# One 512-column product per high weight block: both token parts side by side in the up projections of a split-precision FFN

## The chip, the cores and the metric

The kernel runs on one core of one Trainium2 chip. The metric is the device time of one execution in microseconds (us), lower is better. One number is the median of three runs of the kernel before.

## The reference

Two networks of two layers each run one after the other on one sequence of 256 tokens with model width 1024, all in float32. What matters here are the feed-forward parts:

```
def swiglu(x, w_in, w_out):
    gate, up = jnp.split(x @ w_in, 2, axis=-1)
    return (jax.nn.silu(gate) * up) @ w_out
...
for i in range(DEPTH):                      # first network, DEPTH = 2
    h = x + 0.5 * swiglu(rms_norm(x, norm_ffn1[i]), w_ffn1_in[i], w_ffn1_out[i])   # 1024 -> 2 x 2816 -> 1024
    ... attention and convolution mixer ...
    h = h + 0.5 * swiglu(rms_norm(h, norm_ffn2[i]), w_ffn2_in[i], w_ffn2_out[i])
    ... embedding gate ...
...
for layer in range(DEPTH):                  # second network
    ... three mixers ...
    u = rmsnorm(x, ln2_g[layer]) @ w_up[layer]                                     # 1024 -> 4096
    x = x + jnp.square(jax.nn.relu(u)) @ w_down[layer]                             # 4096 -> 1024
```

So there are four gated feed-forward parts (called ffn1 and ffn2 in each of two layers) and two squared-relu ones (up2 and its down projection).

## The kernel before

**Split precision.** Every large product is made from rounded operands (fp32r) in three pieces: a weight block is split into a high part `whi` and a rest `wlo`, an activation into `x_hi` and `x_lo`, and the product is the sum of `wlo*x_hi`, `whi*x_lo` and `whi*x_hi` in PSUM. The fourth piece, `wlo*x_lo`, is left out.

**Pieces of weight.** The weights arrive as a list of pieces in a fixed order (`plan()`, `NUM[piece]`), mostly 1 MB: four 128-row chunks of 512 columns. The SP queue loads piece n into `raw` (4 buffers). ScalarE makes `whi` of it in `high()` (L998) and VectorE makes `wlo` by a subtraction in `low()` (L1510), both into 4 buffers, three pieces ahead of TensorE (`AHEAD = 3`); `high()` of piece n waits until TensorE has used piece n-4. The order of the work on each engine is written out by hand in the same sequence of stages, and semaphores tie the engines together: `s_used` counts pieces that TensorE has used, `s_hi` and `s_lo` the split ones.

**Up projection.** `columns_` (L520 to L522) takes a 128x128 weight block as the stationary operand and 256 columns (all the tokens) of the transposed activation as the moving one. For each of four chunks of a piece and each of four blocks m it issues the three products, each of 256 columns, into half a bank of PSUM. A unit j consists of two pieces (chunks 0 to 3 and 4 to 7) and fills the two banks of one pair: in the gated parts the first bank holds 2x256 columns of the gate, the second the same of the up value. There are 11 units j in each gated part, and 8 units in each of the two up2 stages (two halves `hf` of 4). The pairs `G0` and `G1` take turns; the pair `P2` and the first bank of `SO` serve as scratch for transposes (`spare`), and the second bank of `SO` for attention values and convolution.

**Behind a unit.** In a gated part VectorE multiplies the gate bank with the row scales (L1610, `s_gate`), ScalarE applies Silu (L1064, `s_silu`), VectorE multiplies with the up bank (L1612, `s_up`); later ScalarE writes `hid_hi` (L1069) and VectorE `hid_lo` (L1618). These instructions stand in the queues between the splits of later pieces. In up2 ScalarE takes the relu out of PSUM (L1422), squares it into `hid_hi` (L1430), and VectorE squares it again (L2136) and subtracts (L2138).

**Down projection and all else.** `rows` (L469 to L471) has the activation as the stationary operand and 512 weight columns as the moving one, in three products as well. The down projections and most of the mixers use it.

**The first stage** has one job more: `bias_of_heads`, a generator that both TensorE and VectorE advance by one at each tick, makes a table (product at L579, VectorE L1592) that goes through a scratch tensor in HBM and returns as `bias` in eight transfers (L2288).

Of the kernel before, what the change touches and what calls it, by code (L numbers as in the profile page):

```python
# [23 lines left out]
AHEAD = 3  # L24
# [152 lines left out]

def hv(name, l, g, t):

    n = NORM[name, l]  # L180
    return 4 * (n - 1) + 4 * ((n > 9) + (n > 11)) + 2 * g + t + 1
# [57 lines left out]
def build(nc, x_d, w_d, c_d, c2_d, rb_d, oh_d, msk_d, pt_d, line_d, out_d):  # L239
    with ExitStack() as ctx:  # L240
# [10 lines left out]
        x_hi = sb("x_hi", [128, 8, 256], F32R)  # L251
        x_lo = sb("x_lo", [128, 8, 256], F32R)
# [38 lines left out]
        PS = [ctx.enter_context(nc.psum_tensor(f"ps{i}", [128, 512], F32)) for i in range(8)]  # L291
        BANKS = {"G0": (PS[0], PS[1]), "G1": (PS[2], PS[3]), "P2": (PS[4], PS[5]), "SO": (PS[6], PS[7])}
        TB = (PS[4], PS[5], PS[6])
        O = PS[7]

# [11 lines left out]
        s_gate, s_silu, s_up, s_hhi, s_hlo = (sem(n) for n in ("s_gate", "s_silu", "s_up", "s_hhi", "s_hlo"))  # L307

        s_relu, s_r2, s_uhi, s_ulo = (sem(n) for n in ("s_relu", "s_r2", "s_uhi", "s_ulo"))
# [22 lines left out]
        s_dv = sem("s_dv")  # L332

# [87 lines left out]
        def tensor(e):  # L421
# [108 lines left out]

            X = (x_hi, x_lo)
# [41 lines left out]
            def bias_of_heads():  # L573

                for _ in range(8):
                    yield
# [5 lines left out]
            def ffn1(l, f, nxt):  # L582
# [11 lines left out]
                for j in range(11):  # L594
                    if j > 1:
                        columns_(u[j][0], bank(f, l, j), f, l)
                    columns_(u[j][1], bank(f, l, j), f, l, mid=(lambda: spread(f, l)) if j == 0 else None)
                    gate_frees(j)
# [320 lines left out]
            def ffn2(l, nxt):  # L919
                H = (F2["hid_hi"], F2["hid_lo"])  # L920
                for hf in range(2):
# [4 lines left out]
                    def relu_frees(j):  # L926
                        free[bks[j]] = [[(s_relu, 2 * (Q + j) + i + 1)] for i in range(2)]

                    columns_(u[0][0], bks[0], "up2", l)
                    if hf == 0:  # L930
                        x_of_h("up2", l, 1)
                    columns_(u[1][0], bks[1], "up2", l)
                    for j in range(4):
                        if j > 1:
                            columns_(u[j][0], bks[j], "up2", l)
                        columns_(u[j][1], bks[j], "up2", l)
                        relu_frees(j)
                    for g in range(2):
                        bk = bks[4 + g]
# [30 lines left out]
        def scalar(e):  # L970
# [84 lines left out]
            def ffn1(l, f, nxt):  # L1055
# [9 lines left out]

                def hid(j):
# [14 lines left out]
                for j in range(11):  # L1081
                    if j > 1:
                        high(NUM[u[j][0]] + AHEAD)
                        hid(j - 1)
                        high(NUM[u[j][1]] + AHEAD)
                    else:
# [92 lines left out]
            def mixer1(l, nxt):  # L1179
# [52 lines left out]
                def sum_turns(g):  # L1232
                    for i in range(2):
# [3 lines left out]
                        e.activation(flat(x_hi[:, c:c + 2, :]), TB[b][:, :], ACT.Copy, scale=0.5).then_inc(s_xhi, 1)  # L1237
# [76 lines left out]
            def x_of_mix(l, c, m):  # L1314
# [3 lines left out]
                e.activation(flat(op[0][:, i:i + m, :]), TB[b][:, 0:256 * m], ACT.Copy,  # L1318
# [92 lines left out]
            def ffn2(l, nxt):  # L1411
                for hf in range(2):
# [3 lines left out]
                    def relu(j):  # L1416
                        for i in range(2):
                            sq = tmp[:, (j % 2) * 1024 + i * 512:(j % 2) * 1024 + i * 512 + 512]
# [3 lines left out]
                            e.activation(sq, BANKS[bank("up2", l, 6 * hf + j)][i][:, :], ACT.Relu).then_inc(s_relu, 1)  # L1422

                    def hid(j):
                        for i in range(2):
# [4 lines left out]
                            e.activation(flat(F2["hid_hi"][:, 4 * j + 2 * i:4 * j + 2 * i + 2, :]), sq, ACT.Square).then_inc(s_uhi, 1)  # L1430
# [4 lines left out]
                    high(NUM[u[1][0]] + AHEAD)  # L1435
                    high(NUM[u[0][1]] + AHEAD)
                    relu(0)
                    high(NUM[u[1][1]] + AHEAD)
                    hid(0)
                    relu(1)  # L1440
                    for j in (2, 3):
                        high(NUM[u[j][0]] + AHEAD)
                        hid(j - 1)
                        high(NUM[u[j][1]] + AHEAD)
                        relu(j)
# [35 lines left out]
        def vector(e):  # L1481
# [52 lines left out]
            def x_low(name, l, lo, hi, T, g, upto):  # L1534

                lo, hi = flat(lo), f32(flat(hi))
# [49 lines left out]
            def bias_of_heads():  # L1586
                for _ in range(8):
# [4 lines left out]
                e.tensor_tensor(T1["line"][:, :], TB[b][0:8, :], T1["msk"][:, :], ALU.add).then_inc(s_lw, 1)  # L1592

            def ffn1(l, f, nxt):
# [6 lines left out]
                def gated(j):  # L1601
                    buf = (j % 2) * 1024
                    gt, pr = tmp[:, buf:buf + 512], tmp[:, buf + 512:buf + 1024]
                    ps = BANKS[bank(f, l, j)]
                    e.wait_ge(s_used, NUM[u[j][1]] + 1)
# [4 lines left out]
                    e.tensor_tensor(two(gt), two(ps[0][:, :]), rsb2, ALU.mult).then_inc(s_gate, 1)  # L1610
                    e.wait_ge(s_silu, 11 * F + j + 1)
                    e.tensor_tensor(pr, ps[1][:, :], gt, ALU.mult).then_inc(s_up, 1)  # L1612
# [508 lines left out]
            def ffn2(l, nxt):  # L2121
# [4 lines left out]
                for hf in range(2):  # L2126
                    Q = 8 * l + 4 * hf
                    u = [halves("w_up_2", l, cols(4 * hf + j)) for j in range(4)]

                    def hid(j):  # L2130
                        for i in range(2):
# [4 lines left out]
                            v = step(e.tensor_tensor(sq, sq, sq, ALU.mult))  # L2136
                            e.wait_ge(s_dv, v)
# [5 lines left out]
                    low(NUM[u[1][0]] + AHEAD)  # L2143
                    low(NUM[u[0][1]] + AHEAD)
                    low(NUM[u[1][1]] + AHEAD)
                    hid(0)
                    for j in (2, 3):
                        low(NUM[u[j][0]] + AHEAD)
                        hid(j - 1)
                        low(NUM[u[j][1]] + AHEAD)  # L2150
                    for g in range(2):
# [8 lines left out]
                        for t in range(2):  # L2160
                            residual(spec, bank("up2", l, 6 * hf + 4 + g), lambda t: rsq(n, t), *nxt, g, back=4 * (hf == 0), ts=(t,))
# [229 lines left out]
```

## Time and profile before

| what | value |
|---|---|
| median of three runs | 1805.46 us (1803.58, 1805.46, 1805.49) |
| profiled execution | 1803.1 us, its span 1801.3 us |
| granted TensorE clock over the span | 0.998 |
| TensorE products (PE) busy | 1780.1 us, 99% |
| TensorE weight loads (PEld) busy | 1617.7 us, 90% |
| VectorE (DVE) busy | 1106.3 us, 61% |
| ScalarE (ACT) busy | 891.7 us, 50% |
| HBM read | 300.02 MB |

The span goes from the first to the last instruction of the profiled execution; 1.8 us of its time lie outside. PE is TensorE's product instructions, PEld its weight loads, which overlap the products. The end of a product in the trace is modelled and products overlap each other in it, so the distance from one start to the next tells what a product costs, and the duration of one row doesn't. A group row gives instructions xcount, busy us, mean ns of one, and the idle time of the engine just before them with what ended it.

### The profile page before, as it was taken

The numbers are of one execution on the slowest core, as the hardware profiler recorded it, in microseconds if no ns is written. First come the engines' busy times: TensorE is split into PE (matmuls) and PEld (weight loads), VectorE is DVE, ScalarE is ACT, GpSimd is POOL, SyncE is SP. The second block draws the span as 40 slices with busy tenths as digits, with TensorE's granted clock in tenths as the row PEclk, the third lists the DMA queues.
The fourth block names the chain that finished last, engine by engine and source line by source line (L and its number), as shares of the span: only waits on it lengthen the run. The fifth ranks groups of instructions, "written<-read, shape, count | busy, mean of one in ns | idle before, by whom it ended". The sixth has DMA issues, their size and how long they took to land.

```text
span 1801.3 us, 28974 instructions
## 1 busy us (share of the span) xinstructions
PE 1780.1 (99%) x11422; PEld 1617.7 (90%) x11422; DVE 1106.3 (61%) x1604; ACT 891.7 (50%) x1304; POOL 26.5 (1%) x32
## 2 busy tenths in 40 slices
PE   9999999999999999999999999999999999999998
PEld 9998898899988999888889998888898988889896
DVE  6555588765555655468775554667565656756554
ACT  5444456544444544355654443566553545645352
POOL 0000000000000000000000000000000000000000
PEclk9999999999999999999999999999999999999999
DMA  8854533555455554543345545534355543435551
GB/s 301 230 180 171 201 117 117 187 174 184 176 178 186 194 181 174 199 166 116 141 164 193 188 169 179 189 114 148 111 192 206 172 169 101 141 103 202 191 184 47
DMA packets 45852, 303.22 MB, mean 168 GB/s; under 512 B 5104, under 2 KB 6256, under 8 KB 12312
## 3 DMA queue, kind: packets, MB, share of 16 engines
q1 hardware_dynamic: 45720, 301.36, 47.9%
q8 instruction: 95, 1.56, 0.4%
q14 instruction: 37, 0.30, 0.0%
HBM read 300.02 MB, written 1.31 MB: 167 GB/s over the span
## 4 chain that ended last, share of the span: by engine, by line
PE 88%; DVE 6%; ACT 4%; issue 3%; POOL 0%; POOLq 0%; DVEq 0%; ACTq 0%
PE ps L469 13%; PE ps L520 13%; PE ps L522 13%; PE ps L521 13%; PE ps L471 13%; PE ps L470 13%; DVE wlo L1510 2%; PE ps L542 2%; PE ps L798 2%; PE ps L616 1%; ACT whi L998 1%; PE ps L822 1%; PE ps L807 1%; PE ps L649 1%; PE ps L789 0%
## 5 line engine op out<-in xcount | busy, mean ns | idle before, releaser
L1510 DVE TENSOR_TENSOR wlo<-raw,whi 128x1024 fp32r<-128x1024 f32 (+4 forms) x388 | 657.2, 1704 | 436.7 <-ACT whi L998 435.5
L998 ACT ACTIVATE whi<-raw 128x1024 fp32r<-128x1024 f32 (+4 forms) x388 | 553.7, 1442 | 357.0 <-PE ps L471 223.9
L520 PE MATMUL ps<-x_hi,wlo 128*128 128x256 f32 x2048 | 582.2, 284 | 1.4 <-DVE wlo L1510 1.4
L522 PE MATMUL ps<-x_hi,whi 128*128 128x256 f32 x2048 | 579.5, 283 | 0.0
L521 PE MATMUL ps<-x_lo,whi 128*128 128x256 f32 x2048 | 579.5, 283 | 0.0
L520 PEld LDWEIGHTS ps<-x_hi,wlo 128*128 128x128 f32 x2048 | 392.9, 192 | 3.1 <-DVE wlo L1510 1.6
L521 PEld LDWEIGHTS ps<-x_lo,whi 128*128 128x128 f32 x2048 | 393.0, 192 | 0.5
L522 PEld LDWEIGHTS ps<-x_hi,whi 128*128 128x128 f32 x2048 | 392.9, 192 | 0.0
L469 PE MATMUL ps<-whi,hid_hi 128*128 128x512 f32 x600 | 233.9, 390 | 0.0
L470 PE MATMUL ps<-wlo,hid_hi 128*128 128x512 f32 x600 | 233.5, 389 | 0.0
L471 PE MATMUL ps<-whi,hid_lo 128*128 128x512 f32 x600 | 233.4, 389 | 0.0
L469 PE MATMUL ps<-whi,x_hi 128*128 128x512 f32 (+3 forms) x544 | 211.4, 389 | 0.6 <-ACT vb L1375 0.6
L471 PE MATMUL ps<-whi,x_lo 128*128 128x512 f32 (+3 forms) x544 | 201.5, 370 | 0.0
L470 PE MATMUL ps<-wlo,x_hi 128*128 128x512 f32 (+3 forms) x544 | 201.2, 370 | 0.0
L471 PEld LDWEIGHTS ps<-whi,hid_lo 128*128 128x128 f32 x600 | 112.6, 188 | 23.5
L470 PEld LDWEIGHTS ps<-wlo,hid_hi 128*128 128x128 f32 x600 | 112.7, 188 | 22.9
L469 PEld LDWEIGHTS ps<-whi,hid_hi 128*128 128x128 f32 x600 | 112.7, 188 | 22.9
L1064 ACT ACTIVATE tmp<-tmp 128x512 f32<-128x512 f32 x44 | 27.8, 632 | 186.4 <-DVE tmp L1610 186.4
L469 PEld LDWEIGHTS ps<-whi,x_hi 128*128 128x128 f32 x544 | 102.8, 189 | 17.6 <-issue 3.5
L471 PEld LDWEIGHTS ps<-whi,x_lo 128*128 128x128 f32 x544 | 102.8, 189 | 15.8
L470 PEld LDWEIGHTS ps<-wlo,x_hi 128*128 128x128 f32 x544 | 102.9, 189 | 14.1
L1674 DVE SCALAR_TENSOR_TENSOR acc<-cpad,cst,acc 128x256 f32<-128x256 f32 x178 | 74.4, 477 | 0.0
(265 smaller groups left out, 1496.2 us busy)
## 6 DMA issues: line engine op xcount, KB each, us to landing
raw<-in_w SPq DMA_DIRECT2D x261, 1024.0 KB, 4.8
raw<-in_w SPq DMA_DIRECT2D x12, 768.0 KB, 4.2
raw<-in_w SPq DMA_DIRECT2D x14, 512.0 KB, 3.4
raw<-in_w SPq DMA_DIRECT2D x4, 576.0 KB, 3.7
raw<-in_w SPq DMA_DIRECT2D x4, 432.0 KB, 3.2
bias<-line_scratch SPq DMA_DIRECT2D x8, 192.0 KB, 9.8
h<-in_x SPq DMA_DIRECT2D x2, 512.0 KB, 5.4
out<-h SPq DMA_DIRECT2D x2, 512.0 KB, 2.7
```

The costliest lines, as they stand in the source:

```text
L469: e.matmul(o, ph, wh, start=first, stop=False)
L470: e.matmul(o, ph, wl, start=False, stop=False)
L471: i = e.matmul(o, pl, wh, start=False, stop=last)
L520: e.matmul(o, wl, x_hi[:, c, :], start=first and n == 0 and m % 2 == 0, stop=False)
L521: e.matmul(o, wh, x_lo[:, c, :], start=False, stop=False)
L522: i = e.matmul(o, wh, x_hi[:, c, :], start=False, stop=last and n == len(spec[2]) - 1 and m % 2 == 1)
L542: ins = e.transpose(o, src[:, t, c * 128:c * 128 + 128], ident)
L798: i = e.matmul(TB[b][:, c0:c0 + w], q[:, t * 128:t * 128 + 128], kk[:, 0:w], start=True, stop=True)
L998: e.activation(w_at(whi, j, off, n), raw[:, j % RAW, off:off + n], ACT.Copy).then_inc(s_hi, count)
L1064: e.activation(gt, gt, ACT.Silu).then_inc(s_silu, 1)
L1510: e.tensor_tensor(w_at(wlo, j, off, n), raw[:, j % RAW, off:off + n], f32(w_at(whi, j, off, n)), ALU.subtract).then_inc(s_lo, count)
L1674: return e.scalar_tensor_tensor(out=a, in0=x, scalar=w, in1=a, op0=ALU.mult, op1=ALU.add)
```

## The change

In all units but the first two of each gated part and the first two of each up2 stage, both token parts of a weight block's work are laid side by side. `x_hi` and `x_lo` become halves of one tensor `x` of 8 chunks x 512 columns (`x_lo` first). A new function `wide_` issues for each block one product of `whi` with all 512 columns, into a whole bank, and one product of `wlo` with the 256 columns of `x_hi`, onto the second half of the same bank. The four blocks of a unit take four banks: units use `P2` and `SO` and the two `G` pairs in turn. The two halves of each bank are added on the way out: ScalarE copies the left halves of two banks to SBUF (`lefts`, in up2 `up`), VectorE adds the right halves (`parts_sum`), and the old steps follow on the sums in SBUF.

In up2 the relu and the square move to one VectorE instruction (`square`), ScalarE's square becomes a copy, and VectorE's second square goes. The second half of up2 no longer crosses its first two units, and the down projection of the first half takes `P2` and `SO`. `bias_of_heads` starts two ticks earlier. Writes into `x` use access patterns of two runs in place of flat ones.

```
+def wide(name, l, j):
+    narrow = {"ffn1": (0, 1), "ffn2": (0, 1), "up2": (0, 1)}[name]
+    if j in narrow:
+        return None
+    if name == "up2":
+        return ("P2", "SO") if j in (2, 5, 7) else (bank(name, l, 0), bank(name, l, 1))
+    return ("P2", "SO") if j % 2 == 0 else (bank(name, l, 1), bank(name, l, 0))
...
+def down_bank(l, hf, g):
+    return ("P2", "SO")[g] if hf == 0 else bank("up2", l, 10 + g)
...
-            out += crossed(u[0], u[1]) + u[2] + u[3]
+            out += (crossed(u[0], u[1]) if hf == 0 else u[0] + u[1]) + u[2] + u[3]
...
+        x = sb("x", [128, 8, 512], F32R)
+        x_lo, x_hi = x[:, :, 0:256], x[:, :, 256:512]
...
+            def wide_(spec, bks, name, l):
+                j = NUM[spec]
+                first, last = spec[2][0] == 0, spec[2][-1] == 7
+                for n, c in enumerate(spec[2]):
+                    e.wait_ge(s_lo, split_value(j, n * 512))
+                    e.wait_ge(s_xlo, xv(name, l, c))
+                    for m in range(4):
+                        if first and n == 0:
+                            for s, v in free[bks[m // 2]][m % 2]:
+                                e.wait_ge(s, v)
+                        o = BANKS[bks[m // 2]][m % 2]
+                        wh, wl = w_at(whi, j, n * 512 + m * 128, 128), w_at(wlo, j, n * 512 + m * 128, 128)
+                        e.matmul(o, wh, x[:, c, :], start=first and n == 0, stop=False)
+                        i = e.matmul(o[:, 256:512], wl, x_hi[:, c, :], start=False, stop=last and n == len(spec[2]) - 1)
+                        if n == len(spec[2]) - 1 and m == 3:
+                            i.then_inc(s_used, 1)
+                    if n % 2 == 1 and n < len(spec[2]) - 1:
+                        tick()
+                tick()
...
             def bias_of_heads():
-                for _ in range(8):
+                for _ in range(6):
                     yield
...
+                def lefts(j):
+                    for i, bk in enumerate(wide(f, l, j)):
+                        out = tmp[:, (j % 2) * 1024 + i * 512:(j % 2) * 1024 + i * 512 + 512]
+                        e.wait_ge(s_used, NUM[u[j][1]] + 1)
+                        e.wait_ge(s_hlo, 11 * F + j - 1)
+                        e.activation(two(out), PAIR[bk][:, :, 0:256], ACT.Copy).then_inc(s_left, 1)
...
+            def parts_sum(out, bk):
+                return step(e.tensor_tensor(two(out), PAIR[bk][:, :, 256:512], two(out), ALU.add))
...
+                        e.wait_ge(s_left, left(F, j, 0))
+                        v = parts_sum(gt, bks[0])
+                        e.wait_ge(s_left, left(F, j, 1))
+                        w = parts_sum(pr, bks[1])
+                        g_in, u_in = gt, pr
+                        e.wait_ge(s_dv, v)
+                    e.tensor_tensor(two(gt), two(g_in), rsb2, ALU.mult).then_inc(s_gate, 1)
                     e.wait_ge(s_silu, 11 * F + j + 1)
-                    e.tensor_tensor(pr, ps[1][:, :], gt, ALU.mult).then_inc(s_up, 1)
+                    if bks is not None:
+                        e.wait_ge(s_dv, w)
+                    e.tensor_tensor(pr, u_in, gt, ALU.mult).then_inc(s_up, 1)
...
+                    def square(j):
+                        w = wide("up2", l, 4 * hf + j)
+                        sq = [tmp[:, (j % 2) * 1024 + i * 512:(j % 2) * 1024 + i * 512 + 512] for i in range(2)]
+                        v = [None, None]
+                        for i in range(2):
+                            e.wait_ge(s_upc, 2 * (Q + j) + i + 1)
+                            if w is not None:
+                                v[i] = parts_sum(sq[i], w[i])
+                        for i in range(2):
+                            if w is not None:
+                                e.wait_ge(s_dv, v[i])
+                            e.scalar_tensor_tensor(out=sq[i], in0=sq[i], scalar=0.0, in1=sq[i], op0=ALU.max, op1=ALU.mult).then_inc(s_relu, 1)
```

## Rows read from the trace of the kernel before

**Rows 1.** The profile page: engines, TensorE's granted clock by slices, chain that ended last.

```profile
PE 1780.1 (99%) x11422; PEld 1617.7 (90%) x11422; DVE 1106.3 (61%) x1604; ACT 891.7 (50%) x1304; POOL 26.5 (1%) x32
PEclk9999999999999999999999999999999999999999
PE 88%; DVE 6%; ACT 4%; issue 3%; POOL 0%; POOLq 0%; DVEq 0%; ACTq 0%
```

**Rows 2.** Stretches, TensorE alone: us, busy (products), granted clock, DMA share, GB/s.

```profile
46.96:133.36 86.40, 86.40 (x722) 1.00 0.68 208
139.20:169.20 30.00, 30.00 (x134) 1.00 0.53 191
1386.95:1433.03 46.08, 46.08 (x386) 1.00 0.54 184
```

**Rows 3.** Instructions in order of time, TensorE: start us, duration us.

```profile
93.04 0.28 PE L520 MATMUL ps<-x_hi,wlo 128*128 128x256 f32 x1
93.16 0.28 PE L521 MATMUL ps<-x_lo,whi 128*128 128x256 f32 x1
93.28 0.28 PE L522 MATMUL ps<-x_hi,whi 128*128 128x256 f32 x1
93.40 0.28 PE L520 MATMUL ps<-x_hi,wlo 128*128 128x256 f32 x1
...
139.12 0.40 PE L469 MATMUL ps<-whi,hid_hi 128*128 128x512 f32 x1
...
169.07 0.39 PE L469 MATMUL ps<-whi,hid_hi 128*128 128x512 f32 x1
```

**Rows 4.** The chain, windows on the convolution and on transposes: start us, us.

```profile
224.72 2.16 PE ps L616 x10
1229.08 1.31 PE ps L789 x12
```

**Rows 5.** Groups of instructions by line and shape, whole span.

```profile
L520 PE MATMUL ps<-x_hi,wlo 128*128 128x256 f32 x2048 | 582.2, 284 | 1.4 <-DVE wlo L1510 1.4
L1422 ACT ACTIVATE tmp<-ps 128x512 f32<-128x512 f32 x32 | 17.4, 595 | 52.5 <-PE ps L522 52.5
L1610 DVE TENSOR_TENSOR tmp<-ps,rsb 128x512 f32<-128x512 f32 x44 | 30.4, 690 | 54.7 <-PE ps L522 54.7
L2136 DVE TENSOR_TENSOR tmp<-tmp 128x512 f32<-128x512 f32 x32 | 21.9, 684 | 0.0
L1575 DVE SCALAR_TENSOR_TENSOR h<-ps,rs_all,h 128x512 f32<-128x512 f32 x32 | 22.7, 744 | 20.8 <-PE ps L497 12.7 <-PE ps L471 8.1
```

**Rows 6.** Instructions in order of time, VectorE, one unit of the first stage.

```profile
93.24 0.69 DVE L1610 TENSOR_TENSOR tmp<-ps,rsb 128x512 f32<-128x512 f32 x1 [1.37 <-PE ps L522]
94.63 0.69 DVE L1612 TENSOR_TENSOR tmp<-ps,tmp 128x512 f32<-128x512 f32 x1 [0.70 <-ACT tmp L1064]
96.50 2.29 DVE L1510 TENSOR_TENSOR wlo<-raw,whi 128x2048 fp32r<-128x2048 f32 x1 [1.18 <-ACT whi L998]
98.71 0.69 DVE L1618 TENSOR_TENSOR hid_lo<-tmp,hid_hi 128x512 fp32r<-128x512 f32 x1
101.10 2.29 DVE L1510 TENSOR_TENSOR wlo<-raw,whi 128x2048 fp32r<-128x2048 f32 x1 [1.70 <-ACT whi L998]
104.76 0.69 DVE L1610 TENSOR_TENSOR tmp<-ps,rsb 128x512 f32<-128x512 f32 x1 [1.37 <-PE ps L522]
```

**Rows 7.** The same unit on ScalarE.

```profile
93.97 0.63 ACT L1064 ACTIVATE tmp<-tmp 128x512 f32<-128x512 f32 x1 [4.49 <-DVE tmp L1610]
94.50 1.90 ACT L998 ACTIVATE whi<-raw 128x2048 fp32r<-128x2048 f32 x1
96.30 0.62 ACT L1069 ACTIVATE hid_hi<-tmp 128x512 fp32r<-128x512 f32 x1
99.08 1.92 ACT L998 ACTIVATE whi<-raw 128x2048 fp32r<-128x2048 f32 x1 [2.16 <-PE ps L522]
```

**Rows 8.** In order of time, first stage: TensorE and VectorE around the table's product.

```profile
28.54 0.28 PE L520 MATMUL ps<-x_hi,wlo 128*128 128x256 f32 x1
...
37.27 1.02 PE L579 MATMUL ps<-oh,rb 32*8 32x512 f32 x2
...
32.70 2.29 DVE L1510 TENSOR_TENSOR wlo<-raw,whi 128x2048 fp32r<-128x2048 f32 x1 [1.18 <-ACT whi L998]
...
40.98 0.67 DVE L1592 TENSOR_TENSOR line<-ps,msk 8x512 f32<-8x512 f32 x1
```

More of the change, by code:

```diff
@@ L289, in build @@
         F2 = scope(4, [("hid_hi", [128, 16, 256], F32R), ("hid_lo", [128, 16, 256], F32R)])
[L291 to L294, printed above, removed]
+        PAIR = {b: ctx.enter_context(nc.psum_tensor(f"ps{b}", [128, 2, 512], F32)) for b in ("G0", "G1", "P2", "SO")}
+        BANKS = {b: (p[:, 0, :], p[:, 1, :]) for b, p in PAIR.items()}
+        TB = (*BANKS["P2"], BANKS["SO"][0])
+        O = BANKS["SO"][1]
         s_raw = [sem(f"s_raw{i}") for i in range(RAW)]
@@ L529, in columns_, with wide_frees @@
                 tick()
+            def wide_(spec, bks, name, l):
[17 more added lines that the diff above has]
+                tick()
+            def wide_frees(bks, *when):
+                for bk, w in zip(bks, when):
+                    for t in range(2):
+                        free[bk][t] = [w]
             X = (x_hi, x_lo)
@@ L594, in ffn1 @@
                 for j in range(11):
[L595 to L598, printed above, removed]
+                    bks = wide(f, l, j)
+                    if bks is None:
+                        columns_(u[j][1], bank(f, l, j), f, l, mid=(lambda: spread(f, l)) if j == 0 else None)
+                        gate_frees(j)
+                    else:
+                        wide_(u[j][0], bks, f, l)
+                        wide_(u[j][1], bks, f, l)
+                        wide_frees(bks, (s_gate, 11 * F + j + 1), (s_up, 11 * F + j + 1))
                 for g in range(2):
@@ L1236, in sum_turns @@
                         e.wait_ge(s_tp, u + 1)
-                        e.activation(flat(x_hi[:, c:c + 2, :]), TB[b][:, :], ACT.Copy, scale=0.5).then_inc(s_xhi, 1)
+                        e.activation(x_hi[:, c:c + 2, :], two(TB[b][:, :]), ACT.Copy, scale=0.5).then_inc(s_xhi, 1)
                 for g in range(2):
@@ L1317, in x_of_mix @@
                 e.wait_ge(s_tp, u + 1)
-                e.activation(flat(op[0][:, i:i + m, :]), TB[b][:, 0:256 * m], ACT.Copy,
+                e.activation(op[0][:, i:i + m, :], TB[b][:, 0:256 * m].rearrange("p (a n) -> p a n", n=256), ACT.Copy,
                              scale=sm[:, 206:207] if c == 6 else 1.0).then_inc(s_xhi, 1)
@@ L1414, in ffn2, with up @@
                     u = [halves("w_up_2", l, cols(4 * hf + j)) for j in range(4)]
-                    def relu(j):
+                    def up(j):
+                        w = wide("up2", l, 4 * hf + j)
                         for i in range(2):
-                            sq = tmp[:, (j % 2) * 1024 + i * 512:(j % 2) * 1024 + i * 512 + 512]
+                            out = tmp[:, (j % 2) * 1024 + i * 512:(j % 2) * 1024 + i * 512 + 512]
                             e.wait_ge(s_used, NUM[u[j][1]] + 1)
@@ L1421, in relu @@
                                 e.wait_ge(s_ulo, 2 * (Q + j - 2) + i + 1)
-                            e.activation(sq, BANKS[bank("up2", l, 6 * hf + j)][i][:, :], ACT.Relu).then_inc(s_relu, 1)
+                            if w is None:
+                                e.activation(out, BANKS[bank("up2", l, 6 * hf + j)][i], ACT.Copy).then_inc(s_upc, 1)
+                            else:
+                                e.activation(two(out), PAIR[w[i]][:, :, 0:256], ACT.Copy).then_inc(s_upc, 1)
                     def hid(j):
@@ L1429, in hid @@
                                 e.wait_ge(s_used, NUM[piece("w_down_2", l, (12, 13, 14, 15), cols(1))] + 1)
-                            e.activation(flat(F2["hid_hi"][:, 4 * j + 2 * i:4 * j + 2 * i + 2, :]), sq, ACT.Square).then_inc(s_uhi, 1)
+                            e.activation(flat(F2["hid_hi"][:, 4 * j + 2 * i:4 * j + 2 * i + 2, :]), sq, ACT.Copy).then_inc(s_uhi, 1)
                     high(NUM[u[0][0]] + AHEAD)
@@ L1434, in ffn2 @@
                         x_of_h("up2", l, 1)
-                    high(NUM[u[1][0]] + AHEAD)
+                        high(NUM[u[1][0]] + AHEAD)
                     high(NUM[u[0][1]] + AHEAD)
[L1437 to L1442, printed above, removed]
+                    up(0)
+                    for j in (1, 2, 3):
+                        if hf == 1 or j > 1:
+                            high(NUM[u[j][0]] + AHEAD)
                         hid(j - 1)
                         high(NUM[u[j][1]] + AHEAD)
-                        relu(j)
+                        up(j)
                     for g in range(2):
@@ L1586, in bias_of_heads @@
             def bias_of_heads():
-                for _ in range(8):
+                for _ in range(6):
                     yield
@@ L1603, in gated @@
                     gt, pr = tmp[:, buf:buf + 512], tmp[:, buf + 512:buf + 1024]
-                    ps = BANKS[bank(f, l, j)]
-                    e.wait_ge(s_used, NUM[u[j][1]] + 1)
+                    bks = wide(f, l, j)
                     if j < 2:
@@ L2160, in ffn2 @@
                         for t in range(2):
-                            residual(spec, bank("up2", l, 6 * hf + 4 + g), lambda t: rsq(n, t), *nxt, g, back=4 * (hf == 0), ts=(t,))
+                            residual(spec, down_bank(l, hf, g), lambda t: rsq(n, t), *nxt, g, back=4 * (hf == 0), ts=(t,))
                             if hf == 1 and nxt == ("final", 0):
```

49 lines of the change are left out of this document (27 added, 22 removed).

## The prediction

> **What bounds the kernel now.** I read the page first. TensorE's products are busy for 99% of the span, the granted clock is full in every slice, and the chain that ended last is 88% TensorE [rows 1]. A busy row is no proof of a bound, because the products overlap each other there, so I looked at distances between starts. In the up projection of the first stage the 256-column products start every 120 ns (93.04, 93.16, 93.28, 93.40) [rows 3], and the windows say that this holds without a break: 86.40 us hold 722 products, two of which began before the window, so 720 at 120.0 ns [rows 2]. An up2 stretch gives the same: 386, less two, in 46.08 us, 120.0 ns [rows 2]. Over the whole span the 2048 first products of a block waited 1.4 us together [rows 5]. So these stages are bound by TensorE's rate of products and by nothing else. VectorE and ScalarE each wait for TensorE once per unit: VectorE stands idle 1.37 us before its gate product, ScalarE 2.16 us before a split [rows 6, 7].
>
> **What a product costs.** In the down projection the 512-column products start at 139.12 and, 132 products later, at 169.07 [rows 3] (the windows hold 134 there, two of them cut by the edges [rows 2]): 29.95 / 132 = 226.9 ns. 256 columns more cost 106.9 ns, which is 2.4 columns per ns at a granted clock of 1.00 (the 2.4 GHz level) [rows 2]. What is left of either distance is 13.1 ns that every product pays whatever its width. That is the whole source of the gain: the change moves exactly as many columns through TensorE as before (768 per block) but in two instructions, not three.
>
> **The sum on TensorE.** A block now costs 3 x 120.0 = 360.0 ns. It will cost 226.9 + 120.0 = 346.9, so 13.1 less. Blocks that change: 9 of 11 units in four gated parts and 6 of 8 in two up2 stages are 36 + 12 = 48 units, each of two pieces with 16 blocks: 1536 of the 2048 blocks [rows 5]. 1536 x 13.1 ns = 20.1 us. A 512-column product whose moving operand is the activation does not occur in the trace. From above its cost is bounded by two of the present products, 240 ns (no gain); from below by the nearest row of something else, the convolution's products at 216 ns [rows 4], which would make the gain 24 x 1536 = 36.9 us. I take 226.9, since L469 has the same number of columns, the same rounded type and a 128x128 stationary block; only which tensor moves differs. Weight loads don't limit the new order: transposes, each with a load of its own, start every 109 ns [rows 4], and one load per 120 or 227 ns has room.
>
> The Trainium skill (TensorE: Matmul & The Clock Gate, Back-to-back issue gap) gives a distance of N/2.4 + 2.5 ns at full clock. By that rule the fixed part is 2.5 ns and the change would save 1536 x 2.5 = 3.8 us. This trace disagrees: 120.0 and 226.9 where the rule gives 109.2 and 215.8.
>
> **What is added on ScalarE and VectorE.** Per gated unit ScalarE makes two copies out of PSUM, bounded by L1422's 0.60 us each, and VectorE two additions with a PSUM operand, 0.69 us each as L1610 [rows 5]. A unit will last 32 x 346.9 ns = 11.10 us. VectorE's busy time in it is 2 x 2.29 + 3 x 0.69 [rows 6] = 6.65 now, 8.03 then; ScalarE's 2 x 1.91 + 0.63 + 0.62 [rows 7] = 5.07 now, 6.3 then. Both fit, but the queue is in order, so the round trip counts. From the end of a unit on TensorE: first copy 0.60, two sums 1.38, hand-overs about 0.1, so the gate product starts 2.1 us later than now. The first `wlo` split begins 3.26 us behind the gate product [rows 6], so at 5.4 and ends at 7.65; the `hid_lo` subtraction ends at 8.3; the second `whi` split must wait for TensorE's first piece (5.55) and for ScalarE, which ends `hid_hi` at 3.68 + 2.1 = 5.8 [rows 7], so it ends at 7.7; the second `wlo` split ends at 10.5 or 10.6. The next gate work is due at 11.10. VectorE's idle 1.37 us shrinks to some 0.5 and nothing piles up.
>
> Even if it did, there is a lead. `high()` and `low()` work three pieces ahead: the split that ends at 96.50 + 2.29 = 98.79 is of the piece behind the three that TensorE takes from 93.04 on, which starts at 93.04 + 3 x 5.76 = 110.32. That is a lead of 11.5 us [rows 3, 6]. It becomes 3 x 5.55 - 7.65 = 9.0 us. The copies, sums and later gate products thus cost TensorE nothing; their cover is these 9 us and the 0.5 us per unit. Banks come back in time: a unit's four banks are wanted again two units on, 11 us after its end, and are free at about 4.3 us (two sums, gate product, Silu, product).
>
> In up2, ScalarE keeps two copies and two splits' worth of work; VectorE loses two squares of 0.68, gains two sums of 0.69 and two fused relu-squares, for which L1575's 0.74 stands [rows 5]: 7.3 us becomes 8.8 of 11.10. The chain is copy 0.6, two sums 1.4, two squares 1.5, first split to 5.8, subtractions to 7.2, second split to 9.5: it fits with more room. The uncrossed order of the second half moves two pieces past each other and no work. The down projection on `P2` and `SO` finds them free for over 11 us, and the next wide unit wants them 11 us after the residual sums begin (two of 0.74). Costs nothing while TensorE is behind that much work; without that cover a bank wait would cost at most the 1.5 us of the two sums, twice.
>
> SP's and the DMA queues' work is the same list; 1 MB per 5.55 us in place of 5.76 raises 208 GB/s to 216, with a DMA share of 0.68 now [rows 2]. The two-run patterns of writes into `x` are on ScalarE and VectorE and of the same size; I take nothing.
>
> **One tight place.** The first wide unit of the first stage needs `P2` and `SO`, and the table's product sits in `SO`. Its VectorE step comes two ticks earlier, right behind the split that ends at 32.70 + 2.29 = 34.99, and takes 0.67: done at 35.66. TensorE's fourth piece begins at 28.54 and takes 5.76 and now the table's 1.02 us too: it ends near 35.3, and the third block, the first to want that bank, comes 0.69 later, at 36.0 [rows 8]. Spare: 0.3 us. A miss costs under 1 us, once.
>
> **Sum.** 1803.1 (the profiled execution, 1801.3 of span and 1.8 around it) - 20.1 = 1783.0. The median of the runs shown is 2.4 above the profiled one, so 1805.5 - 20.1 = **1785.4 us**, 1.1% faster. A change of 0.2% (3.6 us) is about what can be told from none.
>
> **Rivals.**
> - *The fixed part doesn't fall away* (4%): the 13.1 ns belong to each 256 columns of a moving activation. Then the block stays at 360 ns and the time at 1805.5. For it: no wider product of this kind is in the trace. Against: the 512 columns of L469 do not pay it twice [rows 3].
> - *Most of the fixed part stays* (4%): it belongs to something the new order still does as often, say the turn from one bank to the next, and less than a quarter of the 13.1 ns goes: 1800.5 to 1805.5. The Trainium skill's 2.5 ns per product (see above) would make it 1801.7.
> - *The wide product is nearer the convolution's 216* (3%): 1805.5 - 36.9 = 1768.6.
> - *Part of the gain is lost in waits* (5%): VectorE's round trip overruns by little, or banks come late at stage borders; 10 us given back, 1795.
> - *Slower: the round trip on VectorE becomes the bound* (3%). If copies and sums that step over two banks take 2.3 times the flat ones, the 2.0 us of new work on the path become 4.6, the unit's round trip 13.1 us against 11.10. Over nine units 18 us are lost, less the 9 us of lead: 9 us in each of four gated parts, 36 in all, and 1805.5 - 20.1 + 36 = 1821. It decides from about 1.4 us overrun per unit (12.6 - 9.0 = 3.6 us a stage, six stages eat 20.1). Against it: L1610 already reads PSUM in two runs at 0.69 [rows 5].
> - *Forecast* (81%), own range 1782 to 1789.
>
> Range: 1781 to 1791. It leaves out the two ends named above and the half-lost gain. Faster: 81 + 3 + 5 and half of the 4 at the edge, 91%; same 6%; slower 3%.
>
> **What would show it.** In the profile after: products of 512 columns from L-lines of `wide_` starting 227 ns before their partner and that one 120 ns before the next; a gated unit in 11.10 us; 11422 - 1536 = 9886 products; new copies at 0.60 and sums at 0.69; VectorE's idle time before its first sum in place of the gate's; no wait of TensorE in these stages. The prediction is wrong if wide and narrow products come further apart, if TensorE waits for `wlo` late in a gated part, or at the start of a wide unit for a bank.

## The result

The change makes the kernel faster, by half of what was forecast: 1794.52 us median (1793.62 to 1796.19) beside 1805.12 for the kernel before on the same chip. The ratio is 0.9944 with a 95% interval of 0.9927 to 0.9961. The forecast was 1785.4, range 1781 to 1791; the sign was right, and the size lies outside the range.

The page of the profile after: span and engines, then the granted clock by slices, then two groups.

```profile
span 1791.8 us, 26182 instructions
PE 1770.5 (99%) x9886; PEld 1535.6 (86%) x9886; DVE 1159.4 (65%) x1700; ACT 931.8 (52%) x1376; POOL 26.6 (1%) x32
PEclk9999999999999999999999999999999999999999
L569 PE MATMUL psG<-x,whi 128*128 128x512 f32 x704 | 249.7, 399 | 0.0
L544 PE MATMUL psG<-x,wlo 128*128 128x256 f32 x512 | 147.5, 288 | 1.4 <-DVE wlo L1579 1.4
```

The products are 9886, the 11422 of [rows 1] less 1536, as counted. TensorE is at full clock and as busy as before, VectorE and ScalarE rose by 53 and 40 us. TensorE's waits are short and are all in the mixers, at stage starts, or at the very beginning; the window over the wide units of the first stage holds none. The three longest (engine, line, who was waited for; us in total, times, longest us):

```profile
PE psP L845 <- DVE qa L2017: 2.9, 2, 1.4
PE psP L854 <- DVE tmp L2039: 2.5, 2, 1.3
PE psG L544 <- DVE wlo L1579: 1.4, 1, 1.4
```

So the missing 9 us are not in waits. They are in the distance between products. TensorE in order of time, where [rows 3] has the three products of before (start us, duration us):

```profile
92.77 0.40 PE L569 MATMUL psG<-x,whi 128*128 128x512 f32 x1
93.01 0.28 PE L570 MATMUL psG<-x,wlo 128*128 128x256 f32 x1
93.12 0.40 PE L569 MATMUL psG<-x,whi 128*128 128x512 f32 x1
93.36 0.28 PE L570 MATMUL psG<-x,wlo 128*128 128x256 f32 x1
93.47 0.40 PE L569 MATMUL psG<-x,whi 128*128 128x512 f32 x1
93.71 0.28 PE L570 MATMUL psG<-x,wlo 128*128 128x256 f32 x1
93.83 0.40 PE L569 MATMUL psG<-x,whi 128*128 128x512 f32 x1
94.07 0.28 PE L570 MATMUL psG<-x,wlo 128*128 128x256 f32 x1
94.18 0.40 PE L569 MATMUL psG<-x,whi 128*128 128x512 f32 x1
```

The reader is to see the starts of L569: 92.77, 93.12, 93.47, 93.83, 94.18. Four blocks take 1.41 us, 353 ns each, not 346.9. The wide product keeps 0.24 us for itself, the narrow one 0.11 or 0.12. The stretch over all nine wide units of the first stage says that it is everywhere so (us, busy, products, granted clock, DMA share, GB/s):

```profile
35.88:137.63 101.75, 101.75 (x578) 1.00 0.63 199
```

The 578 products are 576 of the wide units and two that the edges of the window cut. 101.75 us for 9 x 32 = 288 blocks are 353.3 ns a block.

What was added behind a unit, on VectorE and then on ScalarE, beside [rows 6, 7]:

```profile
93.31 0.69 DVE L1665 TENSOR_TENSOR tmp<-psP,tmp 128x512 f32<-128x512 f32 x1 [1.73 <-ACT tmp L1129]
93.92 0.68 DVE L1665 TENSOR_TENSOR tmp<-psSO,tmp 128x512 f32<-128x512 f32 x1
94.52 0.68 DVE L1693 TENSOR_TENSOR tmp<-tmp,rsb 128x512 f32<-128x512 f32 x1
95.90 0.69 DVE L1697 TENSOR_TENSOR tmp<-tmp 128x512 f32<-128x512 f32 x1 [0.70 <-ACT tmp L1121]
97.78 2.29 DVE L1579 TENSOR_TENSOR wlo<-raw,whi 128x2048 fp32r<-128x2048 f32 x1 [1.19 <-ACT whi L1055]
99.99 0.69 DVE L1703 TENSOR_TENSOR hid_lo<-tmp,hid_hi 128x512 fp32r<-128x512 f32 x1
100.59 2.29 DVE L1579 TENSOR_TENSOR wlo<-raw,whi 128x2048 fp32r<-128x2048 f32 x1
```

```profile
92.61 0.60 ACT L1129 ACTIVATE tmp<-psP 128x512 f32<-128x512 f32 x1 [3.65 <-PE psSO L570]
93.11 0.59 ACT L1129 ACTIVATE tmp<-psSO 128x512 f32<-128x512 f32 x1
```

The copies take 0.60 us, the sums 0.68 and 0.69, and the second split ends at 102.88, 10.4 us behind the unit's end near 92.5, while the next unit ends at 103.8.

### The profile page after: what moved, and what is told of

The parts are those of the page before. It is cut to its first block, busy times and chain, and to the rows that moved or that the text cites. A ratio compares the mean times of both kernels' runs of the same rounds, so it can differ in the third digit from the quotient of the medians.

```text
span 1791.8 us, 26182 instructions
## 1 busy us (share of the span) xinstructions
PE 1770.5 (99%) x9886; PEld 1535.6 (86%) x9886; DVE 1159.4 (65%) x1700; ACT 931.8 (52%) x1376; POOL 26.6 (1%) x32
## 4 chain that ended last, share of the span: by engine, by line
PE 88%; DVE 6%; ACT 4%; issue 3%; POOL 0%; POOLq 0%; DVEq 0%; ACTq 0%
PE psG L493 12%; PE psG L495 11%; PE psG L494 11%; PE psG L569 9%; PE psP L569 5%; PE psSO L569 5%; PE psG L570 5%; PE psG L544 3%; PE psG L545 3%; PE psG L546 3%; PE psSO L570 3%; PE psP L570 3%; DVE wlo L1579 2%; PE psSO L672 1%; ACT whi L1055 1%
## 5 line engine op out<-in xcount | busy, mean ns | idle before, releaser
L569 PE MATMUL psG<-x,whi 128*128 128x512 f32 x704 | 249.7, 399 | 0.0
L493 PE MATMUL psG<-whi,x 128*128 128x512 f32 (+3 forms) x544 | 211.7, 389 | 0.6 <-ACT vb L1441 0.6
L495 PE MATMUL psG<-whi,x 128*128 128x512 f32 (+3 forms) x544 | 201.5, 370 | 0.0
L494 PE MATMUL psG<-wlo,x 128*128 128x512 f32 (+3 forms) x544 | 201.1, 370 | 0.0
L570 PE MATMUL psG<-x,wlo 128*128 128x256 f32 x704 | 197.7, 281 | 0.0
L493 PE MATMUL psG<-whi,hid_hi 128*128 128x512 f32 x472 | 184.2, 390 | 0.0
L494 PE MATMUL psG<-wlo,hid_hi 128*128 128x512 f32 x472 | 183.7, 389 | 0.0
L495 PE MATMUL psG<-whi,hid_lo 128*128 128x512 f32 x472 | 183.7, 389 | 0.0
L569 PEld LDWEIGHTS psG<-x,whi 128*128 128x128 f32 x704 | 132.3, 188 | 33.1
L569 PE MATMUL psP<-x,whi 128*128 128x512 f32 x416 | 156.4, 399 | 0.0
L569 PE MATMUL psSO<-x,whi 128*128 128x512 f32 x416 | 156.4, 399 | 0.0
L544 PE MATMUL psG<-x,wlo 128*128 128x256 f32 x512 | 147.5, 288 | 1.4 <-DVE wlo L1579 1.4
L545 PE MATMUL psG<-x,whi 128*128 128x256 f32 x512 | 144.8, 283 | 0.0
L546 PE MATMUL psG<-x,whi 128*128 128x256 f32 x512 | 144.8, 283 | 0.0
L493 PEld LDWEIGHTS psG<-whi,x 128*128 128x128 f32 x544 | 102.8, 189 | 17.6 <-issue 3.5
L495 PEld LDWEIGHTS psG<-whi,x 128*128 128x128 f32 x544 | 102.7, 189 | 15.7
```

The costliest lines, as they stand in the source:

```text
L493: e.matmul(o, ph, wh, start=first, stop=False)
L494: e.matmul(o, ph, wl, start=False, stop=False)
L495: i = e.matmul(o, pl, wh, start=False, stop=last)
L544: e.matmul(o, wl, x_hi[:, c, :], start=first and n == 0 and m % 2 == 0, stop=False)
L545: e.matmul(o, wh, x_lo[:, c, :], start=False, stop=False)
L546: i = e.matmul(o, wh, x_hi[:, c, :], start=False, stop=last and n == len(spec[2]) - 1 and m % 2 == 1)
```

## The experiments

All are edits of the changed kernel. The expectations name the possible causes of the missing 6.4 ns a block by letters. A: each change of width from one product to the next has a price. A': the price fades over the products behind the change. B: two products in a row write the same columns of one bank. C: a 512-column product with the activation moving costs more by itself. D: the added work on ScalarE and VectorE disturbs TensorE. E: `whi` and `wlo` take turns. H: every wide product in a mixed stream is slower, however long its run.

"Block" is the time of one 128x128 weight block on TensorE: the distance from a wide product to the one 32 blocks on, divided by 32, median over the 48 units of the one profiled execution. "Pure" is the sum of the distances that each width has in a stream of its own: 120.0 ns for 256 columns, 173.3 for 384 (the mixers' 384-column products in the trace of before start 173 or 174 ns apart), 226.7 for 512. A kernel whose text says "one run", and each of the kernels of other widths, ran once.

**Three products in the new layout.** Four banks, copies and sums stay, the block is three products again.

```
-                        e.matmul(o, wh, x[:, c, :], start=first and n == 0, stop=False)
+                        e.matmul(o[:, 0:256], wh, x_lo[:, c, :], start=first and n == 0, stop=False)
+                        e.matmul(o[:, 256:512], wh, x_hi[:, c, :], start=False, stop=False)
```

> The layout, the four banks and all the added copies and sums of after, but each block again in three products of 256 columns. If the added work on ScalarE and VectorE costs TensorE nothing, as the prediction said, a block is back at 360.0 ns and the time at the kernel before's 1805, within 1.5 us. If the added work disturbs TensorE (theory D: ports or banks shared, waits at stage borders), the block stands above 360 or the time up to 10 us above before.

Measured: 1803.54 us beside 1803.96, ratio 0.9998 (0.9988 to 1.0008), block 360.0. The same stretch as above holds 850 products:

```profile
35.88:137.63 101.75, 101.75 (x850) 1.00 0.64 198
```

850 products, less the two at the edges, are 120.0 ns each. All that was added outside TensorE costs nothing that shows. Theory D, and with it two of the rivals (lost in waits; the round trip as the bound), is out.

**Other bank between the two.** The `wlo` product of a block is issued behind the next block's `whi` product.

```
                         e.matmul(o, wh, x[:, c, :], start=first and n == 0, stop=False)
+                        for n_, c_, m_ in late:
+                            i = e.matmul(BANKS[bks[m_ // 2]][m_ % 2][:, 256:512], w_at(wlo, j, n_ * 512 + m_ * 128, 128), x_hi[:, c_, :], ...)
+                        late = [(n, c, m)]
```

> The wlo product of a block is issued one block later, so that widths still alternate (512, 256, 512, 256) but no two products in a row write the same bank. Theory A (change of width) and C (the wide moving activation) and E (weight tensors in turn): 353.3 ns per block as after, 1794.5. Theory B (same columns of one bank twice in a row): 346.9 ns, 1785.

Measured: block 353.3, 1792.71 us in one run. Theory B is out: with no two products in a row on one bank the block costs the same.

**Both products with 512 columns.**

```
-                        i = e.matmul(o[:, 256:512], wl, x_hi[:, c, :], ...)
+                        i = e.matmul(o, wl, x[:, c, :], ...)
```

> The wlo product too takes all 512 columns and writes the whole bank: it adds wlo*x_lo, a term that the other kernels leave out, and no product in a wide unit changes width. Theory A: two products at 226.9 = 453.8 ns per block, 1536 x 100.5 ns above after, 1949 us. Theory C: 2 x 233.3 = 466.6 ns, 1969 us. Theory B: something near 460 ns, 1959.

Measured: 1946.14 us in one run, block 453.3, so 226.7 per product, with the activation moving and with `whi` and `wlo` taking turns:

```profile
80.02 0.39 PE L569 MATMUL psG<-x,whi 128*128 128x512 f32 x1
80.24 0.39 PE L570 MATMUL psG<-x,wlo 128*128 128x512 f32 x1
80.47 0.39 PE L569 MATMUL psG<-x,whi 128*128 128x512 f32 x1
80.69 0.39 PE L570 MATMUL psG<-x,wlo 128*128 128x512 f32 x1
```

Theories C and E are out: the wide product costs what L469's cost in [rows 3], as long as its neighbours are as wide. The excess needs widths that differ.

**Four by four.** Per chunk four wide products, then their four narrow ones.

```
+                    for m in range(4):
+                        e.matmul(BANKS[bks[m // 2]][m % 2], w_at(whi, ...), x[:, c, :], ...)
+                    for m in range(4):
+                        i = e.matmul(BANKS[bks[m // 2]][m % 2][:, 256:512], w_at(wlo, ...), x_hi[:, c, :], ...)
```

> Per chunk, the four 512-column products of whi are issued first and the four 256-column products of wlo after them; nothing else changes. After costs 353.3 ns per block where 346.9 was forecast. If the 6.4 ns belong to a change of width from one product to the next (theory A), there are 2 changes per chunk in place of 8, a block costs about 348.5 ns and the time is 1536 x 4.8 ns = 7.4 us below after, near 1787. If they belong to two products in a row onto the same columns of one bank (B), none is left: 346.9 ns, 1785. If a 512-column product with the activation moving costs 233 by itself (C): 353.3 and 1794.5 as after. If the two weight tensors taking turns is the cause (E), as A.

Measured: 1787.54 us, ratio 0.9908 (0.9893 to 0.9922), block 350.8. Less than after, but not the 348.5 of a constant price per change: theory A as stated fell too. Three of the four wide distances in a chunk were 233.8 ns on average.

**Sixteen by sixteen.** The same grouping over a whole piece of four chunks.

> Per piece, all sixteen 512-column products first, then all sixteen 256-column ones: 2 changes of width per piece, where four-by-four has 8 and after has 32. Four-by-four measured 1403 ns per chunk of four blocks (pure spacing: 1387), 16.6 ns too much for 2 changes; after is 26.6 ns too much for 8. If the excess belongs to the change and fades behind it (theory A'), a piece has one such excess of 17 ns instead of four: block 347.9 ns, 4.5 us less than four-by-four, ratio to before about 0.988 (1784). If every 512-column product in a mixed stream is slower however long its run (theory H: four-by-four's ran at 234), a block stays at 350.8 and the time at four-by-four's 1787.5 to 1789.

Measured: 1783.70 us, ratio 0.9891 (0.9875 to 0.9908), block 347.9. In the trace, two products to a row, a piece that starts behind narrow products:

```profile
85.02 0.63 PE L568 MATMUL psP<-x,whi 128*128 128x512 f32 x2
85.48 0.62 PE L568 MATMUL psSO<-x,whi 128*128 128x512 f32 x2
85.95 0.62 PE L568 MATMUL psP<-x,whi 128*128 128x512 f32 x2
86.40 0.62 PE L568 MATMUL psSO<-x,whi 128*128 128x512 f32 x2
86.86 0.61 PE L568 MATMUL psP<-x,whi 128*128 128x512 f32 x2
87.31 0.62 PE L568 MATMUL psSO<-x,whi 128*128 128x512 f32 x2
87.76 0.62 PE L568 MATMUL psP<-x,whi 128*128 128x512 f32 x2
88.22 0.62 PE L568 MATMUL psSO<-x,whi 128*128 128x512 f32 x2
88.67 0.40 PE L573 MATMUL psP<-x,wlo 128*128 128x256 f32 x2
88.90 0.40 PE L573 MATMUL psSO<-x,wlo 128*128 128x256 f32 x2
```

The first two pairs take 0.93 us where two later ones (86.86 to 87.76) take 0.90. The single distances behind the change read 233, 236, 228, 233, 231 ns and from the sixth on 226 or 227; the first narrow one behind the wide run is short, 113 or 114 in place of 120, and the second reads 119. So the excess is a run-in of five wide products, some 28 ns, less 8 given back: 20 ns per change, paid once a piece. Theory A' forecast 347.9.

**Two by two.** Groups of two.

> Two 512-column products, then their two 256-column ones: 4 changes per chunk. A constant price per change is already out. A' (an excess that fades behind a change) and H both place a block between after's 353.3 and four-by-four's 350.8, about 352 ns; a block at 346.9 or above 353.3 would speak against both and for a rule of its own in the order of the instructions.

Measured: block 348.3, 1783.44 us in one run. That is nearly as good as sixteen by sixteen and better than four by four, against what was expected: with 4 changes per chunk the block should have lain above 350.8. Its wide distances are 233 ns on average, its narrow ones 115. How much is given back on the narrow products thus depends on the order, and a rule by the number of changes alone doesn't hold.

**Mirrored.** The second piece of a unit starts with its narrow products, so the stream reads 16 wide, 32 narrow, 16 wide.

```
+                (highs if first else lows)()
+                tick()
+                (lows if first else highs)().then_inc(s_used, 1)
```

> As sixteen-by-sixteen, but the second piece of a unit issues its sixteen 256-column products first, so that the stream of a unit is 16 wide, 32 narrow, 16 wide and the next unit goes on wide: one change each way per unit instead of two. Theory A' (an excess of some 20 ns net behind each change to wide that fades within five products): 48 x 20 ns = 1 us below sixteen-by-sixteen, a block at 347.3 ns, ratio to before about 0.9885. Theory H (a mixed stream is slower however long its runs) is out already. If the start of a new bank group behind narrow products had been the cause of the run-in instead, the excess would now be gone at the change in the middle of a unit and stand at the start of units, behind a wide run.

Measured: 1783.74 us, ratio 0.9890 (0.9874 to 0.9907), block 347.3 as forecast. The run-in (234, 235, 229, 232, 231) stands in the middle of a unit, behind narrow products, and is gone at the start of units. The 1 us less is too little to show in the time.

**Other widths, order of after.** Six kernels change one width, four the one of the `whi` product (384, 448, 480, 504 columns) and two the one of the `wlo` product (384, 128). The first has this edit, the others are alike.

```
-                        e.matmul(o, wh, x[:, c, :], ...)
+                        e.matmul(o[:, 128:512], wh, x[:, c, 128:512], ...)
```

> Order of after, but the whi product takes only 384 columns (it leaves out whi*x_lo for the first 128 tokens and leaves the first quarter of each bank unwritten). Pure spacings by the rows of the mixers are 174 and 120 ns, 293.7 per block. If any change of width costs the same, the excess is again 6.6 ns (300.3). If it grows with the difference of the widths, half: 297. If it comes only at 512: 293.7.

> Order of after, the whi product with 448 columns (leaves out whi*x_lo for 64 tokens). 384 + 256 ran at the pure 293.3 ns, 512 + 256 at 353.4 (pure 346.7) and 512 + 384 at 413.3 (pure 400.0). If only a full 512 pays: 320.0 ns. If the excess sets in between 384 and 512: between 320 and 326.

> Order of after, the whi product with 480 columns (leaves out whi*x_lo for 32 tokens). Pure: 213.3 + 120 = 333.3 ns per block. If the excess grows gradually from 448 on (something that fills), half of it, near 336.7. If only the full 512 pays: 333.3.

> The same with 504 columns (leaves out whi*x_lo for 8 tokens). Pure: 223.3 + 120 = 343.3 ns per block. Gradual: near 349. Only the full 512: 343.3.

> Order of after, but the wlo product takes 384 columns (it adds wlo*x_lo for half of the tokens). Pure: 226.7 + 174 = 400.4 ns per block. Any change of width alike: 407. By the difference of the widths: 403.7. If it is the presence of a 256-column product that costs: 400.4.

> Order of after, the wlo product with 128 columns (leaves out wlo*x_hi for half of the tokens). The excess was 6.7 ns beside a 256-column partner and 13.3 beside a 384-column one. If it grows with the width of the narrower partner, it is nearly none here; pure is 226.7 + 66.7 = 293.3 by the columns, or 226.7 + 109 = 336 if a load must fit behind each product. If it were a price of the change of width alone, 6.7 or more on top.

| columns | pure, ns | block, ns | excess | time, us |
|---|---|---|---|---|
| 384 + 256 | 293.3 | 293.3 | 0.0 | 1702.59 |
| 448 + 256 | 320.0 | 320.0 | 0.0 | 1742.03 |
| 480 + 256 | 333.3 | 332.0 | -1.3 | 1760.04 |
| 504 + 256 | 343.3 | 348.0 | +4.7 | 1782.79 |
| 512 + 256 (after) | 346.7 | 353.4 | +6.7 | 1794.52 |
| 512 + 384 | 400.0 | 413.3 | +13.3 | 1883.00 |
| 512 + 128 | 293.3 | 340.0 | +46.7 | 1772.90 |

Pure for 448, 480 and 504 is columns / 2.4 + 13.3 (the 2.4 GHz level, granted clock 1.00). The 413.3 of 512 + 384 is the cost in 40 of its 48 units; the other eight, the second halves of up2, ran at 406.7 (see below). In the trace, 448 with 256 and 512 with 384:

```profile
80.12 0.36 PE L569 MATMUL psSO<-x,whi 128*128 128x448 f32 x1
80.33 0.28 PE L570 MATMUL psSO<-x,wlo 128*128 128x256 f32 x1
80.44 0.36 PE L569 MATMUL psP<-x,whi 128*128 128x448 f32 x1
80.65 0.28 PE L570 MATMUL psP<-x,wlo 128*128 128x256 f32 x1
```

```profile
80.17 0.40 PE L569 MATMUL psG<-x,whi 128*128 128x512 f32 x1
80.41 0.34 PE L570 MATMUL psG<-x,wlo 128*128 128x384 f32 x1
80.58 0.40 PE L569 MATMUL psG<-x,whi 128*128 128x512 f32 x1
80.82 0.34 PE L570 MATMUL psG<-x,wlo 128*128 128x384 f32 x1
```

The first pair repeats every 0.32 us, as pure; the second every 0.41. A change of width alone costs nothing (384 and 448 beside 256). The excess sets in between 480 and 504 columns. It is not a property of the full 512 alone, and 480 is even a little better than pure, which neither guess had. Beside 384 columns it is twice what it is beside 256, in 40 of the 48 units. The row 512 + 128 is a case apart, and its 46.7 ns are not explained. Its 128-column product keeps 60 ns for itself and the wide one 280, and the two weight loads of a block start 108 and 232 ns apart. A bound by weight loads would fit that, but no run tests it. The 109 ns of [rows 4] don't show such a bound: they are plain float32 products of 128 columns, and in the same trace they stay at 109 ns whether the stationary block has 128 columns or 96.

**Weights moving.** The middle product of `rows` takes 256 of its 512 columns.

```
-                        e.matmul(o, ph, wl, start=False, stop=False)
+                        M = 256 if N == 512 else N
+                        e.matmul(o[:, 0:M], ph, wl[:, 0:M], start=False, stop=False)
```

> After with its wide units as they are, but in the down projections and mixers, where weights move and activations stand still, the middle product of each turn of three takes 256 of its 512 columns (leaves out half of the x_hi*wlo term). Pure: 226.7 + 120 + 226.7 = 573.3 ns per turn in place of 680. If the excess behind a change to 512 columns is a property of TensorE's stream whatever moves, a turn costs 580 to 587; if it belongs to the activation as the moving operand, 573.3.

Measured: 1709.46 us in one run. In the down projection a turn of three takes 587 ns (median), pure 573.3 (two 512-column products and a 256-column one):

```profile
140.14 0.40 PE L493 MATMUL psG<-whi,hid_hi 128*128 128x512 f32 x1
140.37 0.28 PE L495 MATMUL psG<-wlo,hid_hi 128*128 128x256 f32 x1
140.50 0.39 PE L496 MATMUL psG<-whi,hid_lo 128*128 128x512 f32 x1
140.72 0.40 PE L493 MATMUL psG<-whi,hid_hi 128*128 128x512 f32 x1
...
141.31 0.40 PE L493 MATMUL psG<-whi,hid_hi 128*128 128x512 f32 x1
```

From 140.14 to 141.31 are two turns, 1.17 us. The excess is there too, so it doesn't depend on which operand moves.

**The same order without the excess.** The trace of this last kernel shows one thing more. Its wide units are those of after, instruction for instruction. In 40 of the 48 the block costs the 353.4 of after. In the eight units of the two second halves of up2, which follow a down projection that now has mixed widths, it costs 346.7, the pure sum, from the fourth product of the half to its end: 230 ns behind each wide product, 116 or 117 behind each narrow one. A stretch of 30 us inside such a half, and one of the same length in the same half of after (us, busy, products, granted clock, DMA share, GB/s):

```profile
1330.00:1360.00 30.00, 30.00 (x175) 1.00 0.51 179
```

```profile
1390.00:1420.00 30.00, 30.00 (x171) 1.00 0.51 176
```

175 less the two at the edges are 173 products, 346.8 ns a pair. After has 233, 117, 241, 120, 236, 113 ns over and over there, 353.3 a pair. The stream in the two kernels differs only in what ran ahead of it: in after the last products of the down projection all have 512 columns. The 512 + 384 kernel shows it too: its second halves of up2, behind a down projection of 512-column products, run at 406.7, its other units, behind 256-column products, at 413.3. So the excess is no fixed price of two widths in turn. One order can run steadily at more than one rate, and which one it takes depends on how the stream was entered. What in the entry decides was not tested.

## Why the prediction was wrong

**What bounds the kernel**: right. TensorE's rate of products sets the time before and after; against the kernel before on the same chip every kernel moved by 1536 times the change of its block, to within about 2.5 us (504 + 256: 4.3 us). Weights moving, which changes other products too, is left aside.

**What a product costs**: right for a uniform stream. The 512-column product with the activation moving takes 226.7 ns when its neighbours have 512 columns too (both-512), and the fixed part of 13.1, rather 13.3 ns, falls away with a product that is merged. The 216 ns taken as the bound from below were no bound: L616's products in the trace of before have 256 columns of plain float32, another width and another type. By the rule of the Trainium skill cited in the prediction (TensorE: Matmul & The Clock Gate, Back-to-back issue gap: N/2.4 + 2.5 ns, which the section gives as the gap of isolated products) the both-512 block would be 2 x 215.8 = 431.7 ns; the trace has 453.3 and disagrees again.

**The sum on TensorE**: this is the step that failed. "It will cost 226.7 + 120.0", 226.9 in the numbers used, took each distance from a stream of its own width and added them. In the mixed stream the block costs 353.3 or 353.4. 1536 x 6.5 ns = 10.0 us; 1785.4 + 10.0 = 1795.4, and 0.9944 x 1805.5 is 1795.4. The mechanism (one product less, one fixed part less) was right and the term was sized 20.1 us where 10.1 came, 1536 x 6.6 ns. The bounds given for the wide product, 216 and 240 ns, did hold its 236; the range gave the likeliest case only a few us of them, and a cost in between was given no case of its own. That was the second mistake: the nearest row shared width and type but not its neighbours. No long stretch of the trace had two widths in turn, but its changes of width showed the excess. The prediction used the row at 139.12 only as the start of an average over 132 products; behind the last 256-column product, at 139.00, the distances begin:

```profile
139.00 0.28 PE L522 MATMUL ps<-x_hi,whi 128*128 128x256 f32 x1
139.12 0.40 PE L469 MATMUL ps<-whi,hid_hi 128*128 128x512 f32 x1
...
140.28 0.39 PE L471 MATMUL ps<-whi,hid_lo 128*128 128x512 f32 x1
```

Five products take 1.16 us where five at 226.7 ns take 1.13. To the nanosecond they are 234, 235, 229, 232 and 231, then 226 or 227: the run-in of sixteen by sixteen, already in the kernel before. It is also why the average read 226.9 and the fixed part 13.1.

**The added work**: right, at 0.60 for the copies and 0.69 for the sums. The forecast had the second split end at 10.5 or 10.6 behind the unit; it ended at 10.4. The fused squares took less than the 0.74 assumed (two in 1.28 us). The three-product kernel shows the whole of it at 0.9998.

**The tight place**: it held. The table's step on VectorE was done at 34.77 + 0.67 = 35.44. The first wide product started at 35.88 without a gap, and the first one to need that bank at 36.59, so 1.1 us were to spare where 0.3 was forecast.

**The rivals**: "the fixed part doesn't fall away" and "most of it stays" had the right place, TensorE's distances, and the wrong cause: the fixed part did go, and half as much came back by another door. The rival "part of the gain is lost in waits" named 1795 and so hit the measured time, but by luck: its waits didn't occur. With the products of a piece grouped the forecast size is there: 0.9891 x 1805.5 = 1785.8.

**What stays open**: why wide products pay behind narrower ones. The runs show that it needs more than 480 columns beside 256, that it fades over five products, and that two products in a row on one bank, `whi` and `wlo` in turn, and the moving operand don't matter. They show that the same alternating order can also run at the pure sum. They don't show what in TensorE does it, what in the entry of a stream picks the rate, nor why two by two gives back nearly as much as sixteen by sixteen.

## What to carry to other kernels

Where TensorE sets the time, count instructions as well as columns: every rounded float32 product in a stream of its own width here paid 13.3 ns on top of its columns, so merging two with the same stationary block gains that much, as long as the evacuation stays in its cover. Don't add up distances measured in uniform streams: read the first products behind each change of width in the trace you have, measure the mixed order, above all next to full 512-column products, and then try to issue the same widths in runs; here moving the narrow products of a piece behind the wide ones, at no other cost, doubled the gain from 0.56% to 1.1%. To see whether added work on other engines costs anything, keep it and put the old products back: one run says it.

## What the runs showed of the hardware that was not expected

- 512-column products in turn with narrower ones mostly cost 6.7 ns per pair more than in a stream of their own beside 256 columns and 13.3 beside 384; 448 and 384 columns beside 256 cost nothing more.
- The same 512 + 256 order ran at 353.4 ns per pair in 40 units and at 346.7 in eight units of one kernel (weights moving), and 512 + 384 at 413.3 and 406.7, depending on the products ahead of the stream.
- Behind narrow products a run of wide ones starts at 233, 236, 228, 233, 231 ns and then keeps 226.7, in the kernel before as well.
- 480 columns beside 256 took 332.0 ns, 1.3 less than the sum of the two pure distances.
